# Moving the first gate slab's products in among the stick-breaking heads of a fused two-block kernel

## The reference, cut to what matters

```
ya = dsa_attention(aq, ak, av, iq, ik, iw, rel_bias) @ w_up_a[l]
yb = stick_breaking_attention(bq, bk, bv) @ w_up_b[l]
yc = memory_attention(cq, mk, mv) @ w_up_c[l]
gates = jax.nn.sigmoid((gate_logits + b_gate[l]).astype(jnp.float32)).astype(x.dtype)
merged = gates[:, :, 0] * ya + gates[:, :, 1] * yb + gates[:, :, 2] * yc
```

```
z = jnp.einsum('bqhd,bkhd->bhqk', q_b, bk).astype(jnp.float32) * HEAD_DIM ** -0.5
log_beta = jax.nn.log_sigmoid(z)
log_one_minus = jnp.where(causal, jax.nn.log_sigmoid(-z), 0.0)
tail = lax.cumsum(log_one_minus, axis=log_one_minus.ndim - 1, reverse=True) - log_one_minus
a = jnp.where(causal, jnp.exp(log_beta + tail), 0.0).astype(bv.dtype)
return jnp.einsum('bhqk,bkhd->bqhd', a, bv)
```

## Time and profile before

| | before |
|---|---|
| median of 3 runs | 1556.53 us (1556.1 to 1556.85) |
| profiled execution, first to last instruction (span) | 1553.7 us |
| what lies around the span, median less span | 2.8 us |
| PE busy | 1529.0 us, 98% of the span |
| DVE / ACT / POOL busy | 703.0 / 601.9 / 693.8 us |
| HBM traffic | 88 GB/s over the span |

### The profile page before, as it was taken

The page is one execution under the profiler, slowest core; times in us unless marked ns, Lnnn a source line. Parts: engine busy times, 40 slices in busy tenths (PEclk is TensorE's granted clock), DMA queues, the critical chain, the costliest instruction groups (busy, mean ns, idle before and its releaser), DMA issues.

```text
span 1553.7 us, 19713 instructions
## 1 busy us (share of the span) xinstructions
PE 1529.0 (98%) x7588; PEld 1253.4 (81%) x7588; DVE 703.0 (45%) x1147; ACT 601.9 (39%) x916; POOL 693.8 (45%) x312
## 2 busy tenths in 40 slices
PE   8999999999999999999999999999999999999898
PEld 7777967877888888888888888888888888887687
DVE  4258855482334226665654005630034346444733
ACT  6353254673332225122221115422444444355452
POOL 6423455334555535443434444444432435454532
PEclk9999999999999999999999999999999999999999
DMA  7314211102333332433332225543422322222021
GB/s 246 122 55 136 82 55 49 41 21 61 102 101 87 109 109 70 118 97 104 85 108 86 104 82 72 99 104 92 126 68 72 101 89 82 95 82 82 28 72 64
DMA packets 145126, 138.26 MB, mean 89 GB/s; under 512 B 7792, under 2 KB 118384, under 8 KB 145052
## 3 DMA queue, kind: packets, MB, share of 16 engines
q1 hardware_dynamic: 140836, 130.79, 29.3%
q10 hardware_dynamic: 4216, 6.45, 1.3%
HBM read 135.09 MB, written 2.13 MB: 88 GB/s over the span
## 4 chain that ended last, share of the span: by engine, by line
PE 90%; DVE 3%; ACT 3%; POOL 2%; issue 1%; DMA 0%; ACTq 0%; DVEq 0%; POOLq 0%
PE banks L732 87%; PE banks L761 2%; POOL w_lo L579 1%; PE banks L920 1%; PE banks L1350 0%; DVE prob L2552 0%; DVE xs L2072 0%; ACT w_hi L1474 0%; POOL prob L721 0%; DMA vec_rows<-in_norm_a 0%; ACT junk L1523 0%; ACT k L1938 0%; POOL prob L723 0%; ACT junk L1762 0%; DVE head_ms L2514 0%
## 5 line engine op out<-in xcount | busy, mean ns | idle before, releaser
L559 POOL TENSOR_TENSOR w_lo<-raw,w_hi 128x2048 fp32r<-128x2048 f32 x104 | 481.4, 4629 | 602.3 <-ACT w_hi L1474 602.3
L732 PE MATMUL banks<-h_hi,w_hi 128*128 128x512 f32 (+1 forms) x904 | 348.1, 385 | 2.4 <-DVE h_lo L2079 0.9
L732 PE MATMUL banks<-h_hi,w_lo 128*128 128x512 f32 (+1 forms) x904 | 340.4, 377 | 0.0
L732 PE MATMUL banks<-h_lo,w_hi 128*128 128x512 f32 (+1 forms) x904 | 340.1, 376 | 0.0
L1474 ACT ACTIVATE w_hi<-raw 128x2048 fp32r<-128x2048 f32 (+2 forms) x123 | 233.1, 1895 | 213.3 <-PE banks L732 203.1
L732 PEld LDWEIGHTS banks<-h_hi,w_hi 128*128 128x128 f32 x904 | 169.9, 188 | 42.1 <-issue 9.7
L732 PE MATMUL banks<-w_hi,h_hi 128*128 128x512 f32 (+1 forms) x544 | 199.8, 367 | 0.0
L732 PE MATMUL banks<-w_hi,h_lo 128*128 128x512 f32 (+1 forms) x544 | 198.2, 364 | 0.0
L732 PE MATMUL banks<-w_lo,h_hi 128*128 128x512 f32 (+1 forms) x544 | 198.1, 364 | 0.0
L732 PEld LDWEIGHTS banks<-h_hi,w_lo 128*128 128x128 f32 x904 | 169.6, 188 | 32.2
L732 PEld LDWEIGHTS banks<-h_lo,w_hi 128*128 128x128 f32 x904 | 169.9, 188 | 29.5
(11 more groups left out here) (319 smaller groups left out, 2348.6 us busy)
## 6 DMA issues: line engine op xcount, KB each, us to landing
raw<-in_w_in SPq DMA_DIRECT2D x56, 512.0 KB, 4.0
raw<-in_w_ffn_in SPq DMA_DIRECT2D x44, 512.0 KB, 5.0
raw<-in_w_in_a SPq DMA_DIRECT2D x32, 512.0 KB, 5.7
raw<-in_w_ffn_out SPq DMA_DIRECT2D x22, 512.0 KB, 4.0
raw<-in_w_ple_gate SPq DMA_DIRECT2D x16, 512.0 KB, 4.6
raw<-in_w_in_b SPq DMA_DIRECT2D x16, 512.0 KB, 4.5
raw<-in_w_out SPq DMA_DIRECT2D x8, 512.0 KB, 4.0
raw<-in_w_out_a SPq DMA_DIRECT2D x8, 512.0 KB, 4.5
```

The costliest lines, as they stand in the source:

```text
L559: pool.tensor_tensor(slot_of(w_lo, slot), slot_of(raw, slot), slot_of(w_hi, slot).bitcast(F32), ALU.subtract).then_inc(lo_made, 1)
L732: return pe.matmul(out, lhsT, rhs, start=start, stop=stop, **kw)
```

## The change

It does the following:

- `stick_pair` writes every pair to bank 0 and waits for the copies of the pair before it. Bank 1 is free from the start of the heads.
- The 12 products of gate slab 0 are computed in bank 1 one or two at a time among the sums and z of steps 1 to 7: first the 8 logits products, then, in the same bank, the 4 up-projection products. ACT copies bank 1 to the new tile `early_logits` after step 4 and to `early_up` after step 7.
- In step 8, 4 logits products of slab 1 take the places that slab 0's had, and the other 4 follow the last sums, all in bank 1. They wait for the copy of `early_up`.
- After the last pair come the logits of slab 2, then slab 1's up-projection (in bank 0) and slab 2's. From slab 3 on all is as before.
- ACT takes slab 0's sigmoid from `early_logits`, DVE multiplies it with `early_up`.

The diff, cut to its core:

```diff
+    early_logits, early_up = (place(n, 99.5 + 2 * a, S) for a, n in enumerate(("early_logits", "early_up")))
...
+        EARLY = BASE["gate"] % 2
+
+        def early_products(first, stop):
+            for n in range(first, stop):
+                if n == 0:
+                    pe.wait_ge(lo_made, BASE["gate"] + 1)
+                    pe.wait_ge(ev_v, EV_V["gate"])
+                if n < KD:
+                    ins = gate_logits(EARLY, 1, n, n + 1)
+                    if n == KD - 1:
+                        ins.then_inc(early_gate_done, 1)
+                else:
+                    if n == KD:
+                        pe.wait_ge(early_out, 1)
+                    ins = gate_up(EARLY, 1, 0, n - KD, n - KD + 1)
+                    if n == KD + 3:
+                        ins.then_inc(slab_used, 1)
...
             pe.wait_ge(st_am, 2 * p + 2)
-            if p >= 2:
-                pe.wait_ge(st_lo, p - 1)
+            if p >= 1:
+                pe.wait_ge(st_lo, p)
...
-                    ins = mm(banks[64 * b:64 * b + 64, p % 2, kt * P:], ...
+                    ins = mm(banks[64 * b:64 * b + 64, 0, kt * P:], ...
...
+        BEFORE_Z = {2: (2, 3), 3: (4, 5), 4: (6, 7), 6: (8, 9), 7: (10, 11)}
+        BEFORE_FIRST = {1: (0, 2), 2: (3, 4), 3: (5, 6), 4: (7, 8), 6: (9, 10), 7: (11, 12)}
         for step in range(1, 8 + 2):
+            early_products(*BEFORE_Z.get(step, (0, 0)))
...
             if step == 8:
-                pe.wait_ge(st_a, 14)
-                gate_logits(wait_slab("gate", 0, 0, 0, 6), 0, 2)
+                pe.wait_ge(early_out, 2)
+                pe.wait_ge(lo_made, BASE["gate"] + 2)
+                gate_logits(1 - EARLY, 1, 0, 3)
...
+                early_products(*BEFORE_FIRST.get(step, (0, 0)))
                 if step == 8:
-                    gate_logits(BASE["gate"] % 2, 2, 3)
+                    gate_logits(1 - EARLY, 1, 3, 4)
...
             if step == 8:
-                gate_slab(0, 0, begun=3)
-
-        pe.wait_ge(st_lo, 3)
-        gate_slab(0, 1, lambda: pe.wait_ge(st_lo, 4))
-        for s in range(2, 6):
+                gate_logits(1 - EARLY, 1, 4, KD)
+
+        slot = wait_slab("gate", 0, 2, 2, 6)
+        gate_logits(slot, 2 * slot, 0, KD)
+        pe.wait_ge(st_lo, 4)
+        gate_up(1 - EARLY, 0, 1, 0, 4).then_inc(slab_used, 1)
+        gate_up(slot, 2 * slot + 1, 2, 0, 4).then_inc(slab_used, 1)
+        for s in range(3, 6):
             gate_slab(0, s)
...
+            if step == 4:
+                act.wait_ge(early_gate_done, 1)
+                act.activation(early_logits[:], banks[:, 1, :], ACT.Copy).then_inc(early_out, 1)
+            if step == 7:
+                act.wait_ge(slab_used, BASE["gate"] + 1)
+                act.activation(early_up[:], banks[:, 1, :], ACT.Copy).then_inc(early_out, 1)
         act.wait_ge(st_r, 16)
         act.preload_act_table_set("sigmoid_and_others")
...
-        for s in range(6):
-            gate_slab(0, s, s > 1)
+        act.wait_ge(early_out, 1)
+        gate_slab(0, 0, False, early_logits[:])
+        gate_slab(0, 1, False, banks[:, 1, :])
+        for s in range(2, 6):
+            gate_slab(0, s)
...
+        dve.wait_ge(early_out, 2)
+        gated(0, 0, early_up[:])
+        gated(0, 1, banks[:, 0, :])
+        for s in range(2, 6):
+            gated(0, s)
```

More of the change, by code:

```diff
@@ L385, in _program @@
     mask_made, offset_made = sem("masks_made"), sem("offset_made")
+    early_gate_done, early_out = sem("early_gate_logits_done"), sem("early_gate_block_copied")
     st_z, st_ln, st_sp, st_r, st_a, st_am, st_pv, st_hi, st_lo = (sem(n) for n in (
@@ L1042, in gate_weights, with gate_logits @@
             return (slot_of(w, slot, 12 * P).rearrange("p (k c) -> p k c", k=12) for w in (w_hi, w_lo))
-        def gate_logits(slot, first, stop):
+        def gate_logits(slot, bank, first, stop):
             hi, lo = gate_weights(slot)
             for k in range(first, stop):
-                mm3(banks[:, 2 * slot, :], hi[:, k], lo[:, k], h_hi[:, k * S:(k + 1) * S], h_lo[:, k * S:(k + 1) * S], k == 0, k == KD - 1)
-        def gate_slab(i, s, up_free=None, begun=0):
-            slot = wait_slab("gate", i, s, s + 6 * i, 6)
[L1051 to L1058, removed]
+                ins = mm3(banks[:, bank, :], hi[:, k], lo[:, k], h_hi[:, k * S:(k + 1) * S], h_lo[:, k * S:(k + 1) * S], k == 0, k == KD - 1)
+            return ins
@@ new lines, in gate_up, with gate_slab @@
+        def gate_up(slot, bank, s, first, stop):
+            hi, lo = gate_weights(slot)
+            for k in range(first, stop):
+                ins = mm3(banks[:, bank, :], hi[:, KD + k], lo[:, KD + k], y_hi[s % 3][:, k * S:(k + 1) * S],
+                          y_lo[s % 3][:, k * S:(k + 1) * S], k == 0, k == 3)
+            return ins
+        def gate_slab(i, s):
+            slot = wait_slab("gate", i, s, s + 6 * i, 6)
+            gate_logits(slot, 2 * slot, 0, KD)
+            gate_up(slot, 2 * slot + 1, s, 0, 4).then_inc(slab_used, 1)
@@ L1086, in stick_pair @@
                     h = 2 * p + b
-                    ins = mm(banks[64 * b:64 * b + 64, p % 2, kt * P:], bv[:, kt * HALF + h * 64:kt * HALF + (h + 1) * 64],
+                    ins = mm(banks[64 * b:64 * b + 64, 0, kt * P:], bv[:, kt * HALF + h * 64:kt * HALF + (h + 1) * 64],
                              stick_a[h % 4][:, TILE_AT[kt]:TILE_AT[kt] + TILE_N[kt]], kt == 0, kt == NT - 1, skip_group_check=True)
@@ L1727, in _, with gate_of, gate_slab @@
                 act.wait_ge(st_pv, pair + 1)
-                act.activation(yb_hi[:, pair * S:(pair + 1) * S], banks[:, pair % 2, :], ACT.Copy).then_inc(st_hi, 1)
+                act.activation(yb_hi[:, pair * S:(pair + 1) * S], banks[:, 0, :], ACT.Copy).then_inc(st_hi, 1)
+            if step == 4:
[4 more added lines that the diff above has]
+                act.activation(early_up[:], banks[:, 1, :], ACT.Copy).then_inc(early_out, 1)
         act.wait_ge(st_r, 16)
         act.preload_act_table_set("sigmoid_and_others")
-        def gate_of(i, s, j, slot):
+        def gate_of(i, s, j, slot, logits=None):
             act.wait_ge(ev_v, EV_V["gate"] + j - 1)
             ft = 2 * i + s // 3
-            act.activation(gate[slot][:], banks[:, 2 * slot, :], ACT.Sigmoid,
+            act.activation(gate[slot][:], banks[:, 2 * slot, :] if logits is None else logits, ACT.Sigmoid,
                            bias=col[:, ds(V_BGATE + KD * (s % 3) + ft, 1)]).then_inc(ev_a, 1)
-        def gate_slab(i, s, split=True):
+        def gate_slab(i, s, split=True, logits=None):
             if split:
@@ L1742, in gate_slab @@
             act.wait_ge(slab_used, g + 1)
-            gate_of(i, s, s + 6 * i, slot)
-        for s in range(6):
-            gate_slab(0, s, s > 1)
+            gate_of(i, s, s + 6 * i, slot, logits)
+        act.wait_ge(early_out, 1)
[3 more added lines that the diff above has]
+            gate_slab(0, s)
         with act.Fori(1, KD // 2) as i:
@@ L2263, in _ @@
                 dve.wait_ge(st_hi, pair + 1)
-                dve.tensor_tensor(yb_lo[:, pair * S:(pair + 1) * S], banks[:, pair % 2, :], yb_hi[:, pair * S:(pair + 1) * S].bitcast(F32),
+                dve.tensor_tensor(yb_lo[:, pair * S:(pair + 1) * S], banks[:, 0, :], yb_hi[:, pair * S:(pair + 1) * S].bitcast(F32),
                                   ALU.subtract).then_inc(st_lo, 1)
-        with dve.Fori(0, KD // 2) as i:
-            for s in range(6):
[L2269 to L2283, removed]
@@ new lines, in gated @@
+        def gated(i, s, up=None):
+            g, slot, _ = at(BASE["gate"], i, s, 6)
+            j, ft, branch = s + 6 * i, 2 * i + s // 3, s % 3
+            dve.wait_ge(ev_a, EV_A["gate"] + j + 1)
+            dst = summed if branch == 0 else term
+            dve.tensor_tensor(dst[:], gate[slot][:], banks[:, 2 * slot + 1, :] if up is None else up, ALU.mult).then_inc(ev_v, 1)
+            dve.wait_ge(ev_v, EV_V["gate"] + j + 1)
+            if branch:
+                dve.tensor_tensor(summed[:], summed[:], term[:], ALU.add).then_inc(merge_step, 1)
+                dve.wait_ge(merge_step, 3 * ft + branch)
+            if branch == 2:
+                hi, lo = merged_hi[:, ds(ft * S, S)], merged_lo[:, ds(ft * S, S)]
+                dve.tensor_copy(hi, summed[:]).then_inc(merge_step, 1)
+                dve.wait_ge(merge_step, 3 * ft + 3)
+                dve.tensor_tensor(lo, summed[:], hi.bitcast(F32), ALU.subtract).then_inc(lo_merged, 1)
+                dve.wait_ge(lo_merged, ft + 1)
@@ L2285, in projection @@
+        dve.wait_ge(early_out, 2)
[3 more added lines that the diff above has]
+            gated(0, s)
+        with dve.Fori(1, KD // 2) as i:
+            for s in range(6):
+                gated(i, s)
         def projection(stage, post, pre, gains_loaded, tiles_before, name):
```

## The result

The changed kernel takes 1566.93 us (5 runs, 1565.2 to 1569.73) against 1556.1 us (5 runs) before: ratio 1.0071, 95% interval 1.0061 to 1.0082. It is slower by 10.8 us, the forecast was 6.8 and its range ended at 1566.0.

A forecast was written before the change was run, and what follows sets the result against it. PE, busy 98% of the span, was taken as the bound, with unchanged work: -3.5 + 0.4 + 1.7 + 3.5 + 4.7 = +6.8 us, a median of 1563.3 us. The range was +3.6 to +9.5 us, 1560.1 to 1566.0.

The forecast's parts named there:

- The heads: Steps 1 to 7: the inserted products fill all of PE's idle time, -3.5 us.
- switching: Eleven more places where PE goes from heads' matmuls to a product and back, 0.04 each, +0.4 us.
- Waits 1, 2 and 3: New PE waits: step 8 on early_up, +1.7; slab 2 on slab 0's multiplication, +3.5; slab 3 on w_lo, +4.7 us.
- The clock: Behind the new waits: whether PE's idle time lowers the array from 2.4 to 1.2 GHz; the sum had nothing for it.
- a rival at 0.14: Clock falls in wait 3 or both long waits, 2.1 us each: +8.9 or +11.0 us; chance 0.14.
- The range: Whole kernel: +3.6 to +9.5 us, 1560.1 to 1566.0, with one fallen clock; about two in ten outside.
- The shared port: Slab 0's multiplication, reading early_up in SBUF, could be held by POOL: nothing in the sum, up to 1.5 us if POOL later.

The follow-up runs named there:

- e5: e2 with slab 1's logits in bank 4, no copy of bank 1 to early_up, two slab 1 products behind the last pair; 0.9989 of the kernel before, -2.1 us.
- e2: The changed kernel with slab 1's up-projection ahead of slab 2's logits; ratio 1.0001 to the kernel before, +0.2 us.
- e1: The changed kernel with 14 idle matmuls ahead of slab 2's wait and 18 ahead of slab 3's; ratio 1.0046 to the kernel before, +7.3 us.
- e6: The changed kernel with 9 idle matmuls ahead of slab 3's wait only; ratio 1.0070 to the kernel before, +10.8 us.
- e9: The changed kernel with 14 idle matmuls ahead of slab 2's wait only; ratio 1.0061 to the kernel before, +9.4 us.
- e3: The changed kernel with slab 0's sigmoid, its table load and multiplication ahead of the last pair's copies; ratio 1.0053 to the kernel before, +8.5 us.

## Why the prediction was wrong

- **The heads** (-3.5, switching +0.4): right. From step 1's z to the first gate matmul of step 8 are now 54.45 us, for 47.28 + 8.17 of before's work and waits with 12 products: 1.0 less. The old waits are gone, and what the new ones leave for switching is -1.0 + 3.5 - 1.7 - 0.3 = 0.5. From step 2's z to step 3's are 6.70 us (305.87 to 312.57), as the 6.6 expected. For step 4 the text expected 6.6 as well, where 5.95 were measured (321.58 to 327.53): step 5 has no product ahead of its z. e5 shows the gain with no long wait beside it.
- **Waits 1, 2 and 3** (1.7, 3.5, 4.7): right in size, in place and in what ends them: 1.67, 3.57 and 4.54 us idle. e2 shows that the order behind the last pair is the cause of waits 2 and 3. Wait 1 stays in e2 and is 0.69 us, as before, once the copy to `early_up` is gone (e5).
- **The clock**: this is the step that failed. The sum -3.5 + 0.4 + 1.7 + 3.5 + 4.7 has nothing for it: it took the matmuls behind each wait at 0.23 us, on the ground that the waits are short and TensorE comes straight from full work. The fall was a rival at 0.14, with 2.1 us for each wait, +8.9 or +11.0. It happened behind both: +1.7 and +2.3 in the trace, 3.6 us by e1 against the changed kernel, so that 6.8 became 10.8. The rival's price was about right and its chance was not. That the price came so near is partly luck: it takes over the length of the slow stretch at the program's start (4.8 us), while the slow stretches here last from 3.1 us (e6, slab 3) to 5.8 (e9, slab 3). The kernel before had no wait of this length to judge from (behind the program's start the longest is 1.3 us), yet the one place where its TensorE had been idle for several microseconds, the program's start, was followed by slow matmuls, and that deserved more weight than the argument against it. The rule of the Trainium skill (TensorE: Matmul & The Clock Gate, "Why this matters for your kernels"), that a long gap between bursts of matmuls takes the array back to the lower level, spoke for it. This trace agrees with it: the granted clock is down to 0.57 in a window behind 4.54 us of idle time.
- **The range**: it held one fallen clock and ended 0.9 us short of the median. Nothing in the text told the longer wait from the shorter one as to the clock, so a fall behind both, +11.0 by its own price, belonged in the range.
- **The shared port**: the sum had nothing for it, rightly: the multiplication took 0.69 us at 366.57, behind POOL's end at 361.21 + 4.52 = 365.73. e3 showed the mechanism that the text described, at a cost of some 0.6 us (a wait of 2.60 us instead of 2.0). The Trainium skill (GPSIMD Engine Reference, the table of engine properties) says that DVE instructions with two SBUF inputs contend with GpSimd, and e3's 3.02 us agree.

## What to carry to other kernels

Work that is moved forward to fill small holes leaves a hole where it stood. Look at what it covered there: here slab 1's matmuls covered a 3.5 us chain over ScalarE and VectorE, and slab 2's 36 matmuls a 7.4 us chain of weights, and the holes filled were worth only 3.5 us. Follow each double-buffered slot from its last use to its next, since finishing a slab late is as dear as starting the next one late. And price a new TensorE wait of several microseconds with the slow matmuls behind it, some 2 us each here; where the wait can't be avoided, matmuls that filled nearly all of it won that back here, and half a fill did not. Removing the wait by another order (e2) was worth far more than filling it (e1): +0.2 us against +7.3.

## What the runs showed of the hardware

- In the stretch of the heads and first gate slabs, idle times of 1.7 us and less left TensorE at 2.4 GHz in all profiles; 3.57 and 4.54 us lowered it each time. At about 2.6 us it went both ways: e3 kept the level, e6 (2.55 us, behind 2.05 us of fill) did not. What decides there stays open, and each profile is one execution.
- The slow stretch behind a wait is not of one length: 6 (e6, slab 3) to 12 (e9, slab 3) matmuls follow each other at 0.42 or 0.43 us, and it can begin 1.5 us after TensorE has resumed (367.37 and 368.83 in the changed kernel) or with its first matmul (363.79 in e6).
- Two of e5's 11 runs, 1556.07 and 1556.2 us, were 2 us over the others, which lie between 1553.62 and 1554.51, with a mean clock of 0.998 against 0.999 and 1.000. That fits a fall in some executions, but no profile of them exists.
